# Two passages into feed-forward stages: norm factors in four rows, weight sums and low parts moved from GpSimd to VectorE, a new order

## The reference, cut to what matters

```python
x = x + gate * (mixed @ w_out)                 # gate only in the first block
h = rmsnorm(x, g) * (1 + scale) + shift        # second block: only rmsnorm(x, g)
x = x + gate_f * (ffn(h @ w_up) @ w_down)      # convolution over tokens, gelu or silu, gating inside

def rmsnorm(x, g):
    return x * lax.rsqrt(jnp.mean(x * x, axis=-1, keepdims=True) + 1e-6) * g
```

## Time and profile before

| | us |
|---|---|
| median of 3 runs (3510.97 to 3522.56) | 3516.84 |
| the profiled execution | 3513.93 |
| its span, first to last instruction | 3512.1 |
| TensorE matmul busy (share of the span) | 3243.4 (92%) |
| VectorE busy | 2276.8 (65%) |
| ScalarE busy | 1279.4 (36%) |
| GpSimd busy | 986.5 (28%) |

### The profile page before, as it was taken

How to read it: one execution, slowest core, us unless ns; L and a number is a source line. 1 busy time by engine, 2 the same in 40 slices (tenths; PEclk the granted TensorE clock), 3 DMA queues, 4 the chain that set the end, 5 groups by cost and what they waited for, 6 DMA issues and landing times.

```text
span 3512.1 us, 37390 instructions
## 1 busy us (share of the span) xinstructions
PE 3243.4 (92%) x14644; PEld 2522.9 (72%) x14644; DVE 2276.8 (65%) x2695; ACT 1279.4 (36%) x1937; POOL 986.5 (28%) x916
## 2 busy tenths in 40 slices
PE   6979998898978989999999999989889989999999
PEld 3657776566766778888887788855447767888887
DVE  5454434786685797776346866667763599988533
ACT  3322111554222443333234433348541344444322
POOL 1310210122352253332010234411653244333101
PEclk9879998999989999999999999989899999999999
DMA  4443344011433422224443344541003422222543
GB/s 143 144 140 118 113 157 168 1 43 48 138 134 97 159 89 80 84 80 157 141 150 115 109 120 145 181 155 49 30 31 127 156 79 90 84 78 77 193 132 126
DMA packets 110920, 391.66 MB, mean 112 GB/s; under 512 B 14391, under 2 KB 17015, under 8 KB 110360
## 3 DMA queue, kind: packets, MB, share of 16 engines
q1 hardware_dynamic: 62120, 218.77, 19.4%
q0 software_dynamic: 48624, 170.49, 14.0%
HBM read 306.30 MB, written 82.90 MB: 111 GB/s over the span
## 4 chain that ended last, share of the span: by engine, by line
PE 60%; DVE 10%; issue 2%; ACT 2%; POOL 2%; DMA 1%; DVEq 0%; POOLq 0%; ACTq 0%
PE PS L363 18%; PE PS L365 18%; PE PS L364 18%; PE PS L3026 1%; DVE HL L320 1%; PE PS L2987 1%; PE PS L3009 1%; POOL Sc L3227 1%; DVE E L3158 1%; DVE QR L1398 1%; ACT HL L304 0%; PE PS L2661 0%; DMA scr_g<-ev 0%; DVE HTf L1668 0%; DVE H L1795 0%
## 5 line engine op out<-in xcount | busy, mean ns | idle before, releaser
L363 PE MATMUL PS<-H,HL 128*128 128x512 f32 x1920 | 769.2, 401 | 57.3 <-DVE H L571 12.2
L320 DVE TENSOR_TENSOR HL<-RAW,HL 128x1024 fp32r<-128x1024 f32 (+1 forms) x442 | 504.1, 1141 | 414.4 <-ACT HL L304 409.8
L365 PE MATMUL PS<-H,HL 128*128 128x512 f32 x1920 | 756.7, 394 | 0.0
L364 PE MATMUL PS<-H,HL 128*128 128x512 f32 x1920 | 754.8, 393 | 0.0
L304 ACT ACTIVATE HL<-RAW 128x1024 fp32r<-128x1024 f32 (+1 forms) x442 | 374.8, 848 | 1005.0 <-PE PS L365 911.5
L363 PEld LDWEIGHTS PS<-H,HL 128*128 128x128 f32 x1920 | 364.5, 190 | 151.8 <-issue 34.8
L365 PEld LDWEIGHTS PS<-H,HL 128*128 128x128 f32 x1920 | 364.7, 190 | 81.8
L364 PEld LDWEIGHTS PS<-H,HL 128*128 128x128 f32 x1920 | 365.2, 190 | 80.1 <-issue 2.9
L363 PE MATMUL PS<-HT,HL 128*128 128x512 f32 x720 | 289.2, 402 | 22.9 <-DVE HL L320 14.6
L365 PE MATMUL PS<-HT,HL 128*128 128x512 f32 x720 | 286.3, 398 | 0.0
L364 PE MATMUL PS<-HT,HL 128*128 128x512 f32 x720 | 284.6, 395 | 0.0
(11 more groups left out here) (377 smaller groups left out, 5417.9 us busy)
## 6 DMA issues: line engine op xcount, KB each, us to landing
RAW<-in_w_up SPq DMA_DIRECT2D x100, 512.0 KB, 3.6
RAW<-in_w_down SPq DMA_DIRECT2D x88, 512.0 KB, 3.6
RAW<-in_w_proj SPq DMA_DIRECT2D x48, 512.0 KB, 3.6
scr_hid<-hidr POOLq DMA_DIRECT2D x36, 512.0 KB, 2.9
HTf<-scr_hid POOLq DMA_DIRECT2D x72, 256.0 KB, 3.7
RAW<-in_w_wmodr SPq DMA_DIRECT2D x32, 512.0 KB, 4.6
RAW<-in_w_wout SPq DMA_DIRECT2D x26, 512.0 KB, 3.7
scr_res<-HTf POOLq DMA_DIRECT2D x48, 256.0 KB, 3.5
```

The source lines that it names most:

```text
L320: e.tensor_tensor(lo, part_source(k, j, x)[0], hi.bitcast(F32), ALU.subtract).then_inc(*k.low.mark(j, x))
L363: e.matmul(out, lh, rh, start=first, stop=False)
L364: e.matmul(out, lh, rl, start=False, stop=False)
L365: return e.matmul(out, ll, rh, start=False, stop=last)
```

## The change

1. **Norm factors in four rows.** A new constant `pick` (128x8, column 3 ones, else zeros). `half_sum` makes four matmuls with a 128x4 window of it as weights, so that row t of a 4x128 PSUM area gets the sums of tokens 128t to 128t+127. `factor` and the root work on `rn`, 4x128, in place of `R2`. A new `half_spread` brings the factors back to 128 rows with four matmuls (weights: a column of the identity, broadcast), into the bank that `scaled` then reads from PSUM. For half 0 it stands in TensorE's order in the middle of tile t = 12, for half 1 after m2(0).
2. **From GpSimd to VectorE:** the weight sums of the first two pairs (`pair_sums(F.pair[0])`, `pair_sums(F.pair[1])`, with a semaphore of their own), the four low parts of t4, and in block two the low parts of the four odd tiles of half 0.
3. **Other order** on ScalarE and VectorE: `first_sum(5)` ahead of b22's high parts, `left_first(0)` earlier, t2's high parts 1 to 3 together, the split of m4(0) ahead of t4's low parts.

```diff
+    e.memset(k.pick[:, :], 0.0).then_inc(*s.dve.mark("pick", 0))
+    e.wait_ge(*s.dve.at("pick", 0))
+    e.memset(k.pick[:, 3:4], 1.0).then_inc(*s.dve.mark("pick", 1))
...
-        x = part(t, u, 4 if t < 2 * O.begun else 0, 8)
+        if t == 12:
+            part(t, u, 0, 4)
+            free = half_spread(k, e, O, free, 0)
+        x = part(t, u, 4 if t < 2 * O.begun or t == 12 else 0, 8)
...
     e.wait_ge(*O.s.dve.at("acc", h, 7))
-    e.matmul(k.PS[:, 6 + h, :], k.ones[:, :], k.acc2[:, h, :], start=True, stop=True).then_inc(*O.s.pe.mark("norm", h))
-    free[6 + h] = [O.s.dve.at("norm", h)]
+    for t in range(4):
+        x = e.matmul(k.PS[0:4, 6 + h, 0:128], k.pick[:, 3 - t:7 - t], k.acc2[:, h, blk(t)], start=t == 0, stop=t == 3)
+    x.then_inc(*O.s.pe.mark("norm", h))
...
+def half_spread(k, e, O, free, h):
+    e.wait_ge(*O.s.dve.at("norm_inv", h))
+    for t in range(4):
+        x = e.matmul(k.PS[:, 6 + h, blk(t)], k.ident[0:4, t:t + 1].to_broadcast([4, 128]), k.rn[:, h, :], start=True, stop=True, skip_group_check=True)
+    x.then_inc(*O.s.pe.mark("spread", h))
+    free[6 + h] = [O.s.dve.at("o", 7, h)]
+    return free
...
-    e.tensor_scalar(k.R2[:, :], k.PS[:, 6 + h, :], 1.0 / 1024, EPS, ALU.mult, ALU.add).then_inc(*s.dve.mark("norm", h))
+    e.tensor_scalar(k.rn[:, h, :], k.PS[0:4, 6 + h, 0:128], 1.0 / 1024, EPS, ALU.mult, ALU.add).then_inc(*s.dve.mark("norm", h))
...
-    e.reciprocal(k.R2[:, :], k.R2[:, :]).then_inc(*s.dve.mark("norm_inv", h))
+    e.reciprocal(k.rn[:, h, :], k.rn[:, h, :]).then_inc(*s.dve.mark("norm_inv", h))
...
-    e.wait_ge(*s.dve.at("norm_inv", h))
+    e.wait_ge(*s.pe.at("spread", h))
...
-    e.scalar_tensor_tensor(x, x, O.gcol(i), k.R2[:, :], ALU.mult, ALU.mult).then_inc(*s.dve.mark("o", i, h))
+    e.scalar_tensor_tensor(x, x, O.gcol(i), k.PS[:, 6 + h, :], ALU.mult, ALU.mult).then_inc(*s.dve.mark("o", i, h))
...
         pre2(i)
+        if i == 0:
+            free = half_spread(k, e, O, free, 1)
...
     act_block(k, e, O, "t2", 0)
-    act_block(k, e, O, "t2", 1)
     first_sum(3)
     split_high_by(k, e, pre[2])
-    act_block(k, e, O, "t2", 2)
-    act_block(k, e, O, "t2", 3)
+    for q in range(1, 4):
+        act_block(k, e, O, "t2", q)
     first_sum(4)
     split_high_by(k, e, pre[3])
     for q in range(4):
         act_block(k, e, O, "t1", q)
+    first_sum(5)
     for q in range(4):
         act_block_rest(k, e, O, "b22", q)
-    first_sum(5)
...
-    split_high_by(k, e, pre[5])
+    split_high(k, e, F.pair[0], k.pieces.index[pre[5]])
     for q in range(4):
         act_block_rest(k, e, O, "t4", q)
+    split_high_by(k, e, pre[5])
...
     split_low_by(k, e, pre[2])
+    left_first(0)
     dve_block(k, e, O, 2)
     dve_block_low(k, e, O, "t2", 1)
+    pair_sums(k, e, F.pair[0])
     dve_block(k, e, O, 3)
     dve_block_low(k, e, O, "t2", 2)
-    left_first(0)
     split_low_by(k, e, pre[3])
...
         if q:
-            low_rest(k, e, O, "t3", q - 1, O.s.dve)
-    split_low_by(k, e, pre[4])
-    low_rest(k, e, O, "t3", 3, O.s.dve)
+            dve_block_low(k, e, O, "t3", q - 1)
+        if q == 2:
+            split_low_by(k, e, pre[4])
+    dve_block_low(k, e, O, "t3", 3)
     second_sum(0)
     for q in range(4):
         dve_block_rest(k, e, O, "t4", q)
+    split_low(k, e, F.pair[0], k.pieces.index[pre[5]])
+    for q in range(4):
+        dve_block_low(k, e, O, "t4", q)
+    pair_sums(k, e, F.pair[1])
     split_low_by(k, e, pre[5])
...
 def pool_up(k, e, F):
-    s, O = F.s, F.O
-    pair_sums(k, e, F.pair[0])
-    pair_sums(k, e, F.pair[1])
-    for q in range(4):
-        low_rest(k, e, O, "t4", q, O.s.pool)
+    s = F.s
```

More of the change, by code:

```diff
@@ L235, in load_weights @@
             elif before == "first":
-                e.wait_ge(*k.sums.at(b + 1, "s4"))
+                e.wait_ge(*sums_of(k, b + 1).at(b + 1, "s4"))
                 if (b + 1, "m2") in k.pieces.index:
@@ L242, in load_weights, with sums_of @@
         k.next_load += 1
+def sums_of(k, j):
+    return k.sums_dve if j in (*k.F1.pair[:2], *k.F2.pair[:2]) else k.sums
 def pair_sums(k, e, j):
+    signal = sums_of(k, j)
     a, b, SX = k.RAW[:, (j - 1) % N_RAW, :], k.RAW[:, j % N_RAW, :], k.SX
@@ L252, in pair_sums @@
         e.wait_ge(*k.low.at(before, "m5"))
[L253 to L256, removed]
+    e.tensor_tensor(SX[:, 0, :], b[:, 0:512], b[:, 512:1024], ALU.add).then_inc(*signal.mark(j, "s1"))
+    e.wait_ge(*signal.at(j, "s1"))
+    e.tensor_tensor(SX[:, 1, :], SX[:, 0, :], a[:, 0:512], ALU.subtract).then_inc(*signal.mark(j, "s2"))
+    e.tensor_tensor(b[:, 0:512], a[:, 0:512], b[:, 0:512], ALU.subtract).then_inc(*signal.mark(j, "s3"))
     if before:
         e.wait_ge(*k.low.at(before, "m3"))
-    e.wait_ge(*k.sums.at(j, "s2"))
-    e.tensor_tensor(SX[:, 2, :], a[:, 512:1024], SX[:, 1, :], ALU.subtract).then_inc(*k.sums.mark(j, "s4"))
+    e.wait_ge(*signal.at(j, "s2"))
+    e.tensor_tensor(SX[:, 2, :], a[:, 512:1024], SX[:, 1, :], ALU.subtract).then_inc(*signal.mark(j, "s4"))
 def part_source(k, j, x):
@@ L1610, in half_sum @@
         e.wait_ge(*x)
+    e.wait_ge(*k.start.dve.at("pick", 1))
     e.wait_ge(*O.s.dve.at("acc", h, 7))
-    e.matmul(k.PS[:, 6 + h, :], k.ones[:, :], k.acc2[:, h, :], start=True, stop=True).then_inc(*O.s.pe.mark("norm", h))
-    free[6 + h] = [O.s.dve.at("norm", h)]
-    return free
-def low_on_pool(O, i):
-    return O.shcol is None and i % 2 == 1
+    for t in range(4):
+        x = e.matmul(k.PS[0:4, 6 + h, 0:128], k.pick[:, 3 - t:7 - t], k.acc2[:, h, blk(t)], start=t == 0, stop=t == 3)
+    x.then_inc(*O.s.pe.mark("norm", h))
+    return free
+def half_spread(k, e, O, free, h):
[5 more added lines that the diff above has]
+    return free
 def act_halves(k, e, O):
@@ L1629, in act_halves @@
             e.wait_ge(*s.dve.at("norm", 0))
-            e.activation(k.R2[:, :], k.R2[:, :], ACT.Sqrt).then_inc(*s.act.mark("norm", 0))
+            e.activation(k.rn[:, 0, :], k.rn[:, 0, :], ACT.Sqrt).then_inc(*s.act.mark("norm", 0))
         if t >= 12:
@@ L1676, in low @@
     def low(i):
-        if not low_on_pool(O, i):
-            e.wait_ge(*s.act.at("hi", i, 0))
-            less(e, O, i, H[:, 1, i, 0:512], res(k, i, 0), H[:, 0, i, 0:512].bitcast(F32)).then_inc(*s.dve.mark("lo", i, 0))
+        e.wait_ge(*s.act.at("hi", i, 0))
+        less(e, O, i, H[:, 1, i, 0:512], res(k, i, 0), H[:, 0, i, 0:512].bitcast(F32)).then_inc(*s.dve.mark("lo", i, 0))
     for t, (n, h) in enumerate(O.seq):
@@ L1709, in pool_halves @@
 def pool_halves(k, e, O):
[L1710 to L1715, removed]
+    s = O.s
     for t, (n, h) in enumerate(O.seq):
@@ L1723, in pool_halves @@
             store_res(k, e, O, t - 3)
[L1724 to L1727, removed]
+    for t in range(13, 16):
+        store_res(k, e, O, t)
 def store_res(k, e, O, t):
@@ L1961, in act_up @@
     e.wait_ge(*O.s.dve.at("norm", 1))
-    e.activation(k.R2[:, :], k.R2[:, :], ACT.Sqrt).then_inc(*O.s.act.mark("norm", 1))
+    e.activation(k.rn[:, 1, :], k.rn[:, 1, :], ACT.Sqrt).then_inc(*O.s.act.mark("norm", 1))
     split_high_by(k, e, pre[0])
@@ L3415, in build @@
         stages = [k.start, k.qkv, k.att1, k.hyena, k.out1, k.ffn1, k.mid, k.proj2, k.att2, k.branch, k.out2, k.ffn2]
-        k.high, k.low, k.sums = Signal(sem("weights_high")), Signal(sem("weights_low")), Signal(sem("weights_sums"))
+        k.high, k.low = Signal(sem("weights_high")), Signal(sem("weights_low"))
+        k.sums, k.sums_dve = Signal(sem("weights_sums")), Signal(sem("weights_sums_dve"))
         landed = []
@@ L3455, in build @@
         k.small = keep("small", [128, NSMALL])
-        k.ident, k.ones = keep("ident", [128, 128]), keep("ones", [128, 128])
+        k.ident, k.ones, k.pick = keep("ident", [128, 128]), keep("ones", [128, 128]), keep("pick", [128, 8])
         k.modx, k.modc, k.gsc = keep("modx", [128, 48]), keep("modc", [128, 16]), keep("gsc", [128, 40])
@@ L3551, in build @@
         k.F2 = Up(k.ffn2, "up2", "down2", True, None, k.O2, names.index("up2"))
-        signals = [x for s in stages for x in (s.pe, s.act, s.dve, s.pool)] + [k.high, k.low, k.sums] + landed
+        signals = [x for s in stages for x in (s.pe, s.act, s.dve, s.pool)] + [k.high, k.low, k.sums, k.sums_dve] + landed
         def programs(pe, act, dve, pool, sp):
```

21 lines of the change are left out of this document (7 added, 14 removed).

## The result

The changed kernel takes 3530.15 us (median of 7, 3524.55 to 3532.65), the kernel before 3513.28 on the same chip (median of 7, 3510.97 to 3522.56): ratio 1.0043, 95% interval 1.0033 to 1.0054. It is 17 us slower, outside the predicted range of 3509 to 3527. The profiled execution took 3532.65 us, its span is 3530.8.

A forecast was written before the change was run, and what follows sets the result against it. It took each passage to be as long as VectorE's list up to u4(0)'s end. With u4(0) 0.3 us later in each, 2 x 0.3 = 0.6 on 3516.84 gave 3517.4 us, range 3509 to 3527.

The forecast's parts named there:

- part four: VectorE's list from unit 5's split to u4(0)'s end: 37.1 us, before 36.4; u4(0) ends 0.3 later.
- What bounds the passage: In the passage, VectorE's list up to u4(0) sets the length; m4(0) waits for u4(0)'s end.
- Part one: Half 0's narrow factor: TensorE waits 1.6 us in t = 12, spreads for 1.1, waits 0.5 for bank 6.
- Part three: Start of VectorE's bound list: the split of unit 5 begins 0.4 us earlier than before.
- 7.9 us of slowing: VectorE's list in the passage: slowing by GpSimd at t1's and t4's low parts, all of it removed.
- added 7.4: VectorE's list in the passage: eight weight sums, 5.0 us, and t4's four low parts, 2.4.
- net wait: VectorE's list in the passage: added waits for ScalarE's high parts, net 1.2 us.
- The stall of about 7: TensorE reaches m4(0) at about 1247 and waits some 7 us in one piece.
- Sum of the passages: Two passages at 0.3 us later each, 0.6 us in all; forecast chance 0.74.
- rival 1: Clock stays low after the stall at m4(0) and the wait at t = 12: up to 9.6 us in all; chance 0.12.
- Rival 2: VectorE's slowing in the passage belongs to the operations themselves: 17.9 us a passage, 36 in all, slower; chance 0.05.
- Rival 3: m4(0) doesn't wait for VectorE's list, TensorE sets the end: 28 us less in all, 5 more of clock; chance 0.09.

The follow-up runs named there:

- experiment 1: Kernel before with 32 unused bytes a partition ahead of the stage tensors, no instruction changed: 3530.35 us, ratio 1.0040; with 64 bytes 3518.2 us, ratio 1.0006.
- (4): Changed kernel with `pick` at the far end of SBUF, so nothing else moved, against the kernel before: 3514.62 us, ratio 0.9996.
- (5): Nothing moved in SBUF, against the kernel before: moves and new order with 128-row factors, 3507.72 us, 0.9972; changed kernel with u4(0) early, 3514.97 us, 1.0001.
- experiment 8: Changed kernel with 160 bytes of padding behind `pick`, stage tensors at a multiple of 512 bytes from HL, against the kernel before: 3492.72 us, ratio 0.9938.

## Why the prediction was wrong

**The step that failed** is the last sentence of part four, where `pick` is costed: "The two memsets of `pick` at the start lie under the first loads." I priced the instructions of the new constant and not its 32 bytes. The term that is missing from the sum is its place: it moves the stage tensors from 64 to 96 past a multiple of 256, and that is 14.8 us by the padding alone (experiment 1), against 16.9 for the change, and the loss is gone when `pick` lies elsewhere (4). None of the three rivals held this, so neither the range nor the chance of 0.12 for slower could.

The rest, step by step:

- *What bounds the passage*: right. m4(0) (1257.10) still starts right after u4(0) (1256.31, 0.68 long). But "only the moment of u4(0)'s end counts" was too narrow: with u4(0) early the whole list still set the end (5).
- *Part one*: waits of 1.17 and 0.49 (forecast 1.6 and 0.5), sum 0.97 and spread 1.08 from start to start (0.9 and 1.1 forecast; the Trainium skill's figure of 55.8 ns a pass, "TensorE: Matmul & The Clock Gate", gave 0.89 for either, 0.08 and 0.19 less than measured), reciprocal 0.94 (0.93). The lower bound of 0.54 for a sum or spread doesn't follow from the working given: eight records in 0.61 with a tail of 0.27 taken off are 0.04 each, not 0.07; what was measured is near the upper bound. The second norm sum comes 3.6 us later than before (1202.90 - 1171.18 = 31.72 after 28.11), where 3.2 was forecast.
- *Part three*: the split of unit 5 starts at 49.11 from the first norm sum, 0.4 later than before instead of 0.4 earlier: 0.4 of the difference is part one's. The other 0.4 is in the products behind a sum and behind a spread, taken at 0.227 a matmul: 12 of them take 2.97 from 1203.87 to 1206.84, and 48 take 11.02 from 1207.92 to 1218.94, 0.25 and 0.14 more. That the gain ahead of it would go to the spread was right and is now shown: without the narrow factor the split starts 4.7 earlier (5).
- *Part four*: from the start of the split to the end of u4(0) 36.7 us, forecast 37.1. Four subtractions of 128x512 take 2.49 at both places, four weight sums 2.53, so the 7.9 us of slowing are gone with GpSimd's work and the added 7.4 cost what they should. The net wait is 0.6 (1.10 in one piece, 0.50 before), not 1.2.
- *The stall of about 7*: 6.95.
- *Sum of the passages*: +0.7 and +2.0 for +0.3 each. In the first, parts one and three were taken too short by 0.8 and part four too long by 0.4; that these cancel in part is luck. The second has the clock's 1.4 besides (rival 1). The change without its place is 0.7 us faster than the kernel before by the medians, interval -4.6 to +2.1, so "no change by measure" held for what was priced.
- *Rival 1, the clock*: it came, and small. In the six microseconds from m4(0) on the granted clock is 0.58, 0.55 before: a stall of 6.95 in place of 4.32 kept the lower level no longer. In the second passage, after the wait at the first spread, seven matmuls ran at 0.43 us:

```profile
2806.00:2812.00 6.00, 5.90 (x22) 4.79 (x23) 0.26 (x2) 0.15 (x1) 0.00 (x0) 0.72 0.24 88
2812.00:2818.00 6.00, 6.00 (x29) 4.94 (x28) 4.94 (x8) 3.24 (x5) 0.55 (x1) 1.00 0.21 62
```

  The granted clock is 0.72 in the first stretch, with both levels in it, and 1.00 in the next; that is 7 x 0.2 = 1.4 us. In the first passage the same wait cost nothing: from the spread to the bank's wait, 1176.35 to 1199.97, all ran at full pace. In the changed kernel of experiment 8 it is the other way round: the clock falls to 0.80 behind the first passage's spread, m4(0) comes 87.45 after the norm sum, and the second passage has 85.03. So this wait took the clock down in one passage of the two, not always in the same one. By the Trainium skill's "TensorE: Matmul & The Clock Gate" (What's actually happening) the throttled clock is the default that activity releases; these rows agree in that the fall follows a gap and ends during dense work.
- *Rival 2, the slowing stays*: refuted by 2.49 for four subtractions at both places. By the Trainium skill ("SBUF — State Buffer", Who interferes with whom) VectorE and GpSimd can hold each other up; here they did, 1.43 for 0.60.
- *Rival 3, TensorE sets the end*: didn't occur.

Not settled: why the place matters. The Trainium skill ("SBUF — State Buffer", Who interferes with whom) gives TensorE's moving operand and its weight load read ports of their own and knows of contention between VectorE and GpSimd alone; the runs show that the place of an operand costs TensorE up to 8 ns a matmul, so there is more to it than that rule has. The paddings move the stage tensors both against HL and H and in absolute address, and no run here separates the two. Nor does a run tell whether TensorE's two reads disturb each other or another engine's or a transfer's access disturbs them. It isn't known either what tips a down product at place 64 into one pace or the other, nor which conflict the 2 to 8 ns are. Waits in the stages between the blocks, which differ by 1 to 3 us between profiles of one kernel, weren't studied.

## What to carry to other kernels

Price a new tensor by where it lies too: list what the allocator puts behind it, and when TensorE's busy time rises at full clock without an idle gap, divide a dense stretch by its matmul count before looking for a wait. Try a few paddings (here the moving operand at a multiple of 256 bytes from the stationary one was the best of five places), and test any edit that allocates with its padding held equal. A list of work that sets the end wasn't shortened by reordering here: take work off it, and off what gates its first item.

## What the runs showed of the hardware that was not expected

An fp32r matmul of 128x512 in a dense row takes 226.7 ns with HT or `hsr` as the moving tensor at a multiple of 256 bytes from the weights, and 228.9 to 234.6 at four other places, at a granted clock of 1.00: up to 3.5%, and 0.64% of this kernel for 192 bytes of padding. A dense product can fall into one of two paces, 228.9 or 233.3 ns, in the same program and keep it for its 1056 matmuls. A moving tensor that stays where it was is affected as well: H,HL between products with HT goes from 229.8 to 229.0, 227.6 and 226.7 as HT moves to places 96, 128 and 0 and H and HL stay, while in the output product, without HT, it is 226.7 in every kernel.
